# Relative-position bias of a two-layer encoder: stored backward, loaded once, read backward

## Chip, cores and metric

One core of a Trainium2 chip runs the whole kernel as one program. The metric is the device time of one execution in microseconds; the figure compared is the median of several executions.

## What is computed

The reference is two layers of a streaming encoder on 512 tokens of width 1024. Each layer has a feed-forward block, a token mixer with three branches (gated DeltaNet, RG-LRU, chunked band attention), a cross-attention and a second feed-forward block, with a layer norm behind each. The change touches band attention:

```
rel = kj - LA_PAST * CHUNK - qi
bias = rel_table[:, clip(rel, -REL_CLIP, REL_CLIP) + REL_CLIP]     # rel_table (8 heads, 257)
valid = (arange(n)[:, None] - LA_PAST + kj // CHUNK) >= 0
s = where(valid, q @ k.T * 64 ** -0.5 + bias, NEG_INF)
p = softmax(s, axis=-1)
o = p @ v
```

A query adds to each score one entry of its head's table, chosen by the distance from query to key. For a tile of 128 queries (on the partitions) and the 256 keys that end with the tile's own, the bias is a Toeplitz matrix: row q is the table, shifted by q. For keys farther back it is one constant per head.

## The kernel before

Weights come as a stream of units of 128x1024 fp32, four slots deep. SyncE issues the loads. GpSimd splits each unit into a high part (L592) and a low part (L589), and every large product is three matmuls (high by high, low by high, high by low). GpSimd splits the unit for a slot only when `unit_begun` says that the unit behind the slot's former one has begun; the first matmul of each unit on TensorE raises it.

All waits are semaphores written out by hand, and each engine runs its list in order.

In the mixer TensorE computes the projections of queries, keys and values (`att_qk`, `att_v`), turns a few gate rows into columns (L850), and then runs band attention: 8 heads by 4 tiles of queries, n = 0 to 31. It keeps two scores ahead: in turn it issues score n + 2, a quarter of an LRU projection (`lru_part(n + 1)`), and the transposes of the probabilities of n (`turn(n)`, L879). Before the loop stand score 0, score 1 and `lru_part(0)`. Score n reuses the bank of score n - 2 and waits until VectorE has added the bias to that one (`biased`, L1886 and L1884).

VectorE runs, in this order: the memset and the softplus of the gate rows (`delta_rows`, 4x512), two copies of the turned columns (L1996, L1997), the softplus of the LRU rates (`lru_rates_out`, L1924 to L1926, on 128x4 tiles `lam`, the helper at L1837 to L1849), and then its part of attention. `link` puts a wait of the engine for its own last instruction behind an instruction.

The bias tile is made on the device. In layer norm 0 ScalarE's queue loads the gate weights (512 KB), `ba_w` (256 KB) and the table into `ext` (8 KB). VectorE pads `ext` on the left with its first entry (L1853). ScalarE's queue stores `ext` to DRAM (L1705), waits, and loads it back with overlapping rows: partition p of `bias` begins p entries further on, 1 MB in all (L1707). That puts the rows in reversed order, so TensorE multiplies by a flipped identity (L859), into four banks of `aux`, and the banks are copied back over `bias`, two by VectorE (L1859) and two by ScalarE (L1405). VectorE then writes the mask into a corner of the tile (L1863).

Of the kernel before, what the change touches and what calls it, by code (L numbers as in the profile page):

```python
# [41 lines left out]
CH = SEQ // P  # L42
REL = 128
ALPHA = (2 * DEPTH) ** 0.25
LN_EPS = 1e-5
# [131 lines left out]

C_ID, C_CAUSAL, C_FLIP, C_LEVEL = 0, P, 2 * P, 3 * P
CONST = (3 + LEVELS) * P

# [178 lines left out]

def trunk(nc, xT, memT, stream, par_d, ba_w_d, gate_w_d, table_d, const_d, ext_d, outT):  # L360
    with ExitStack() as ctx:
        def sem(name):
            return ctx.enter_context(nc.semaphore(name))

        def sb(name, shape, dt=F32, scope=ctx):
            return scope.enter_context(nc.sbuf_tensor(name, shape, dt))
# [27 lines left out]
        with ExitStack() as mix:  # L394
# [11 lines left out]
            with ExitStack() as att:  # L406
                aq = sb("aq", [P, KB, SEQ], F32, att)
                ak = sb("ak", [P, KB, SEQ], F32, att)
                av = sb("av", [P, CH, BRW], F32, att)
                bias = sb("bias", [P, HA, 2 * P], F32, att)  # L410
                ext = sb("ext", [HA, 3 * P - 1], F32, att)
                sc = sb("sc", [P, CH, SEQ], F32, att)
                pt = sb("pt", [P, CH, SEQ], F32, att)
                neg_max = sb("neg_max", [P, HA * CH], F32, att)
                row_sum = sb("row_sum", [P, HA * CH], F32, att)
                inv_sum = sb("inv_sum", [P, HA * CH], F32, att)
                lc = sb("lc", [P, KB, SEQ], F32, att)
# [39 lines left out]

        ba_w = sc[:, 0, :].rearrange("p (k m) -> p k m", k=KD)
        row_f = pt[0:HN, 0, :]
        tt = tmp[3].rearrange("p (c m) -> p c m", c=CH)  # L460

        ident = const[:, C_ID:C_ID + P]
        flip = const[:, C_FLIP:C_FLIP + P]
        causal = const[:, C_CAUSAL:C_CAUSAL + P]

        def level_mask(s):
# [5 lines left out]
        const_loaded, par_loaded = sem("const_loaded"), sem("par_loaded")  # L472
        mix_par_loaded = [sem(f"mix_par_loaded{n}") for n in range(3)]
        ext_stored, bias_loaded, mem_loaded, out_stored = sem("ext_stored"), sem("bias_loaded"), sem("mem_loaded"), sem("out_stored")
        unit_loaded = [sem(f"unit_loaded{s}") for s in range(SLOTS)]
# [21 lines left out]

        ext_padded = Signal(sem("ext_padded"), 1)
        bias_flipped, bias_copied, bias_copied_late = (
            Signal(sem(n), c) for n, c in (("bias_flipped", 4), ("bias_copied", 2), ("bias_copied_late", 2)))  # L500
        bias_masked = Signal(sem("bias_masked"), 1)
# [114 lines left out]
        def _(pe):  # L616
            def mm(out, w, x, start=True, stop=True):
                return pe.matmul(out, w, x, start=start, stop=stop, skip_group_check=True)  # L618
# [205 lines left out]
            def attention(l):  # L824
# [31 lines left out]

                pe.wait_ge(bias_loaded, l * 16 + 16)
                for m in range(4):
                    mm(aux[:, m, :], flip, bias[:, 2 * m:2 * m + 2, :]).then_inc(bias_flipped.sem, 1)  # L859
                pe.wait_ge(bias_copied.sem, bias_copied.at(l, 2))  # L860

                def score(n):
# [7 lines left out]
                def turn(n):  # L870

                    h, i = divmod(n, CH)
                    pe.wait_ge(probs.sem, probs.at(l, n + 1))
                    if n < 2:
                        pe.wait_ge(bias_copied_late.sem, bias_copied_late.at(l, n + 1))
                    if n >= 2:
                        pe.wait_ge(turned_out.sem, turned_out.at(l, n - 1))
                    for j in range(i + 1):
                        last = pe.transpose(aux[:, 2 + n % 2, j * P:(j + 1) * P], sc[:, i, j * P:(j + 1) * P], ident)  # L879
                    last.then_inc(turned.sem, 1)  # L880
# [436 lines left out]
        def _(act):  # L1317
# [71 lines left out]
            def attention(l):  # L1389
# [13 lines left out]

                for m in range(2):
                    act.wait_ge(bias_flipped.sem, bias_flipped.at(l, m + 3))  # L1405
                    fn(bias[:, 2 * m + 4:2 * m + 6, :], aux[:, m + 2, :].rearrange("p (h k) -> p h k", h=2),
                       ACT.Copy).then_inc(bias_copied_late.sem, 1)

                def turned_copy(n):
# [275 lines left out]
            def mixer_loads(l):  # L1685
                act.dma_start(gate_w[:, :, :, :], gate_w_d[l]).then_inc(mix_par_loaded[0], 16)
                act.dma_start(ba_w, ba_w_d[l]).then_inc(mix_par_loaded[1], 16)
                act.dma_start(ext[:, P - 1:3 * P - 1], table_d[l][:, 0:2 * P]).then_inc(mix_par_loaded[2], 16)

# [5 lines left out]
            for l in range(DEPTH):  # L1695
# [7 lines left out]

                act.wait_ge(ext_padded.sem, ext_padded.at(l, 1))
                act.dma_start(ext_d, ext[:, :]).then_inc(ext_stored, 16)  # L1705
                act.wait_ge(ext_stored, l * 16 + 16)
                act.dma_start(bias[:, :, :], bass.AP(tensor=ext_d.tensor, offset=0,  # L1707
                                                     ap=[[1, P], [3 * P - 1, HA], [1, 2 * P]])).then_inc(bias_loaded, 16)
                attention(l)
# [15 lines left out]
        def _(dve):  # L1725
# [125 lines left out]
            def attention(l):  # L1851
                dve.wait_ge(mix_par_loaded[2], l * 16 + 16)
                dve.tensor_copy(ext[:, 0:P - 1], ext[:, P - 1:P].broadcast_to([HA, P - 1])).then_inc(ext_padded.sem, 1)  # L1853
                lru_rates(l)
                delta_rows(l)
                lru_rates_out(l)
                for m in range(2):
                    dve.wait_ge(bias_flipped.sem, bias_flipped.at(l, m + 1))
                    dve.tensor_copy(bias[:, 2 * m:2 * m + 2, :], aux[:, m, :].rearrange("p (h k) -> p h k", h=2)).then_inc(bias_copied.sem, 1)  # L1859
                dve.wait_ge(bias_copied.sem, bias_copied.at(l, 2))  # L1860
                dve.wait_ge(bias_copied_late.sem, bias_copied_late.at(l, 2))

                dve.memset(bias[0:P // 2, :, 3 * P // 2:2 * P], NEG).then_inc(bias_masked.sem, 1)  # L1863
                dve.wait_ge(bias_masked.sem, bias_masked.at(l, 1))
# [376 lines left out]
def pack(x, mem, ln_g, ln_b, ffn_w12, ffn_w3, mix_w_in, dn_conv_w, dn_a_log, dn_dt_bias, dn_norm_w, lru_conv_w,  # L2241
# [77 lines left out]
    i = np.arange(P)  # L2319
    const = [np.eye(P), i[:, None] <= i[None, :], np.eye(P)[::-1]]  # L2320
    for s in range(LEVELS):
        b = 1 << s
        const.append((i[:, None] // b % 2 == 0) & (i[None, :] // b == i[:, None] // b + 1))
    return {"in_xT": np.ascontiguousarray(A(x)[0].T), "in_memT": np.ascontiguousarray(A(mem)[0].T),
            "in_stream": np.concatenate(stream, 0), "in_par": np.stack(par), "in_ba_w": np.stack(ba),
            "in_gate_w": np.stack(gw), "in_table": A(la_rel_bias), "in_const": np.concatenate(const, 1).astype(np.float32)}

# [14 lines left out]
```

## Time and profile before

| | |
|---|---|
| median of 3 executions | 3166.64 us (3164.72 to 3166.77) |
| profiled execution, first to last instruction | 3165.2 us |
| what lies between that span and the median | 1.4 us |
| TensorE busy | 3110.6 us (98%) |
| VectorE busy | 1471.4 us (46%) |
| ScalarE busy | 720.8 us (23%) |
| GpSimd busy | 1736.3 us (55%) |
| mean granted TensorE clock | 0.992 |

One execution was recorded. Times are microseconds from the span's start, unless marked ns. In a profile PE is the matmul side of TensorE and PEld its weight load, DVE is VectorE, ACT is ScalarE, POOL is GpSimd, SP is SyncE; a name such as ACTq is the engine's DMA queue. The two layers repeat each other some 1571 us apart. L618, L1321 and L1735 are lines of helpers, which stand for all matmuls, all activations and all low parts; there the names of the tiles tell the operations apart.

### The profile page before, as it was taken

The page shows a single profiled execution, that of the slowest core. Times are in us where ns is not written, and L with a number is a line of the kernel's source. Part 1 is how long each engine was busy: PE and PEld are TensorE (multiplying, and loading weights), DVE is VectorE, ACT ScalarE, POOL GpSimd, SP SyncE. Part 2 cuts the span into 40 slices and gives each one's busy share as a digit, 9 for nine tenths or more (in the row PEclk, how much of TensorE's full clock was granted, in tenths as well). Part 3 has the DMA queues.
Part 4 walks back from the last instruction along what each step waited for, and adds up shares of the span by engine and source line. Part 5 has one row for each costly group of instructions (what it writes and reads, how often), then busy time and mean ns, then how long its engine had stood idle before and what let it go on. Part 6 is the DMA issues. An engine that isn't in the chain of part 4 may idle for free.

```text
span 3165.2 us, 42772 instructions
## 1 busy us (share of the span) xinstructions
PE 3110.6 (98%) x15968; PEld 2593.9 (82%) x15968; DVE 1471.4 (46%) x2202; ACT 720.8 (23%) x1433; POOL 1736.3 (55%) x987
## 2 busy tenths in 40 slices
PE   8999999999999999999999999999999999999998
PEld 7888875788888979888888888667888889788887
DVE  3332367755536336332244314677555472353323
ACT  1110224422221423110121103134222224231102
POOL 6666553433346745666656665535333567456664
PEclk9999999999999999999999999999999999999999
DMA  4323221211122322333322332212111224222332
GB/s 155 99 94 106 97 94 40 74 54 54 57 83 87 127 74 87 93 99 100 100 91 96 99 100 92 92 41 74 61 54 51 86 90 130 70 86 94 99 100 67
DMA packets 81173, 272.79 MB, mean 86 GB/s; under 512 B 8433, under 2 KB 16913, under 8 KB 81041
## 3 DMA queue, kind: packets, MB, share of 16 engines
q1 hardware_dynamic: 75808, 264.27, 25.7%
q10 hardware_dynamic: 5088, 5.96, 0.6%
q8 instruction: 100, 1.64, 0.2%
q0 software_dynamic: 144, 0.66, 0.1%
q14 instruction: 33, 0.26, 0.0%
HBM read 268.73 MB, written 2.12 MB: 86 GB/s over the span
## 4 chain that ended last, share of the span: by engine, by line
PE 94%; DVE 3%; ACT 1%; issue 1%; DMA 0%; SPq 0%; ACTq 0%; DVEq 0%
PE acc L618 82%; PE aux L618 12%; PE aux L879 1%; DVE xf L1819 0%; DVE xl L1735 0%; DVE xf L1816 0%; DMA xf<-in_xT 0%; DVE ml L1735 0%; ACT xf L1321 0%; PE aux L1249 0%; DVE xf L1760 0%; DVE y_sum L1774 0%; ACT tmp L1321 0%; ACT xh L1321 0%; DVE lr L2056 0%
## 5 line engine op out<-in xcount | busy, mean ns | idle before, releaser
L589 POOL TENSOR_TENSOR wl<-raw,wh 128x1024 fp32r<-128x1024 f32 x496 | 1213.8, 2449 | 80.1 <-ACT wh L1321 40.1
L592 POOL TENSOR_SCALAR wh<-raw 128x1024 fp32r<-128x1024 f32 x480 | 523.3, 1090 | 1314.2 <-PE acc L618 901.0
L618 PE MATMUL acc<-xh,wh 128*128 128x512 f32 (+1 forms) x2688 | 1016.8, 383 | 17.9 <-ACT xh L1321 15.1
L618 PE MATMUL acc<-xh,wl 128*128 128x512 f32 (+1 forms) x2688 | 987.2, 372 | 0.0
L618 PE MATMUL acc<-xl,wh 128*128 128x512 f32 (+1 forms) x2688 | 948.2, 371 | 0.0
L618 PEld LDWEIGHTS acc<-xh,wh 128*128 128x128 f32 x2688 | 512.9, 191 | 127.0 <-issue 38.7
L618 PEld LDWEIGHTS acc<-xh,wl 128*128 128x128 f32 x2688 | 513.4, 191 | 79.1 <-issue 1.9
L618 PEld LDWEIGHTS acc<-xl,wh 128*128 128x128 f32 x2688 | 488.2, 190 | 87.8
L1735 DVE TENSOR_TENSOR hl<-tmp,hh 128x512 f32 x88 | 238.4, 2709 | 81.8 <-ACT hh L1321 81.8
L618 PE MATMUL acc<-hl,wh 128*128 128x512 f32 (+1 forms) x704 | 264.5, 376 | 0.0
L618 PE MATMUL acc<-hh,wl 128*128 128x512 f32 (+1 forms) x704 | 264.5, 376 | 0.0
L618 PE MATMUL acc<-hh,wh 128*128 128x512 f32 (+1 forms) x704 | 264.5, 376 | 0.0
L1760 DVE SCALAR_TENSOR_TENSOR xf<-acc,xf 128x512 f32<-128x512 f32 (+1 forms) x72 | 43.4, 602 | 399.7 <-PE acc L618 399.4
L1746 DVE TENSOR_TENSOR tmp<-tmp,acc 128x512 f32<-128x512 f32 x88 | 60.5, 688 | 327.5 <-PE acc L618 326.5
L1321 ACT ACTIVATE hh<-tmp 128x512 f32 x88 | 56.0, 637 | 466.3 <-DVE tmp L1746 466.3
L618 PEld LDWEIGHTS acc<-hh,wl 128*128 128x128 f32 x704 | 132.5, 188 | 24.2
L618 PEld LDWEIGHTS acc<-hh,wh 128*128 128x128 f32 x704 | 132.5, 188 | 24.2
L618 PEld LDWEIGHTS acc<-hl,wh 128*128 128x128 f32 x704 | 132.5, 188 | 23.9
L618 PEld LDWEIGHTS aux<-tmp 128*128 128x128 f32 x1088 | 138.8, 195 | 10.5 <-DVE tmp L2151 3.0
L618 PE MATMUL aux<-tmp 128*128 128x128 f32 x1088 | 139.9, 278 | 0.7 <-DVE tmp L2151 0.3
L1321 ACT ACTIVATE tmp<-acc 128x512 f32<-128x512 f32 x96 | 57.4, 598 | 336.0 <-PE acc L618 336.0
L1743 DVE SCALAR_TENSOR_TENSOR tmp<-tmp,acc 128x512 f32<-128x512 f32 x88 | 60.5, 687 | 147.3 <-ACT tmp L1321 147.3
(287 smaller groups left out, 3912.6 us busy)
## 6 DMA issues: line engine op xcount, KB each, us to landing
raw<-in_stream SPq DMA_DIRECT2D x496, 512.0 KB, 3.3
xf<-in_xT SPq DMA_DIRECT2D x2, 1024.0 KB, 10.5
bias<-rel_scratch ACTq DMA_DIRECT2D x2, 1024.0 KB, 6.0
mraw<-in_memT ACTq DMA_DIRECT2D x2, 1024.0 KB, 5.8
out_xT<-xf SPq DMA_DIRECT2D x16, 128.0 KB, 1.7
gate_w<-in_gate_w ACTq DMA_DIRECT2D x2, 512.0 KB, 5.5
const<-in_const POOLq DMA_DIRECT2D x1, 640.0 KB, 6.6
sc<-in_ba_w ACTq DMA_DIRECT2D x2, 256.0 KB, 5.7
```

The costliest lines, as they stand in the source:

```text
L589: pool.tensor_tensor(wl[:, s, :], raw[:, s, :], wh[:, s, :].bitcast(F32), ALU.subtract).then_inc(unit_split, 1)
L592: pool.tensor_scalar(wh[:, s, :], raw[:, s, :], 1.0, 0.0, ALU.mult, ALU.add).then_inc(hi_step, 1)
L618: return pe.matmul(out, w, x, start=start, stop=stop, skip_group_check=True)
L879: last = pe.transpose(aux[:, 2 + n % 2, j * P:(j + 1) * P], sc[:, i, j * P:(j + 1) * P], ident)
L1321: return act.activation(out, in_, func, **kw)
L1735: return tt_(dst, whole, high.bitcast(F32), ALU.subtract)
L1743: stt_(tmp[1][:, :], tmp[0][:, :], 1.0, acc[:, 2 * m, :], ALU.add, ALU.mult).then_inc(freed_d.sem, 1)
L1746: tt_(tmp[2][:, :], tmp[1][:, :], acc[:, 2 * m + 1, :], ALU.mult).then_inc(freed_d.sem, 1)
L1760: evicted = stt_(xf[:, d, t], half_bank(norm, d, half)[:, t], factor, xf[:, d, t], ALU.mult, ALU.add)
```

## The change

The host lays the table out already padded on the left and back to front: `TABLE` = 383 entries per head. One load with overlapping rows, issued in layer norm 0 in the place of the table's load, puts partition p at entry p onward into `bias_back`. `bias` becomes a view of that tile with a negative step on the last axis, so it reads like the old tile. The left padding, the store to DRAM and the load back, the four flipping matmul calls of a layer (which the trace shows as eight matmuls) and the four copies are gone, with their semaphores. The flipped identity leaves the constants (640 to 576 KB). The mask's memset is at the mirrored corner. A filler tile takes the place of `ext`.

```diff
-C_ID, C_CAUSAL, C_FLIP, C_LEVEL = 0, P, 2 * P, 3 * P
-CONST = (3 + LEVELS) * P
+C_ID, C_CAUSAL, C_LEVEL = 0, P, 2 * P
+CONST = (2 + LEVELS) * P
...
-                bias = sb("bias", [P, HA, 2 * P], F32, att)
-                ext = sb("ext", [HA, 3 * P - 1], F32, att)
+                bias_back = sb("bias_back", [P, HA, 2 * P], F32, att)
+                sb("att_fill", [P, 384], F32, att)
...
+        bias = bias_back[:, :, ::-1]
...
-                pe.wait_ge(bias_loaded, l * 16 + 16)
-                for m in range(4):
-                    mm(aux[:, m, :], flip, bias[:, 2 * m:2 * m + 2, :]).then_inc(bias_flipped.sem, 1)
-                pe.wait_ge(bias_copied.sem, bias_copied.at(l, 2))
-
...
-                    if n < 2:
-                        pe.wait_ge(bias_copied_late.sem, bias_copied_late.at(l, n + 1))
...
-                for m in range(2):
-                    act.wait_ge(bias_flipped.sem, bias_flipped.at(l, m + 3))
-                    fn(bias[:, 2 * m + 4:2 * m + 6, :], aux[:, m + 2, :].rearrange("p (h k) -> p h k", h=2),
-                       ACT.Copy).then_inc(bias_copied_late.sem, 1)
...
-                act.dma_start(ext[:, P - 1:3 * P - 1], table_d[l][:, 0:2 * P]).then_inc(mix_par_loaded[2], 16)
+                act.dma_start(bias_back[:, :, :], bass.AP(tensor=table_d.tensor, offset=l * HA * TABLE,
+                                                          ap=[[1, P], [TABLE, HA], [1, 2 * P]])).then_inc(bias_loaded, 16)
...
-                act.wait_ge(ext_padded.sem, ext_padded.at(l, 1))
-                act.dma_start(ext_d, ext[:, :]).then_inc(ext_stored, 16)
-                act.wait_ge(ext_stored, l * 16 + 16)
-                act.dma_start(bias[:, :, :], bass.AP(tensor=ext_d.tensor, offset=0,
-                                                     ap=[[1, P], [3 * P - 1, HA], [1, 2 * P]])).then_inc(bias_loaded, 16)
...
-                dve.wait_ge(mix_par_loaded[2], l * 16 + 16)
-                dve.tensor_copy(ext[:, 0:P - 1], ext[:, P - 1:P].broadcast_to([HA, P - 1])).then_inc(ext_padded.sem, 1)
                 lru_rates(l)
                 delta_rows(l)
                 lru_rates_out(l)
-                for m in range(2):
-                    dve.wait_ge(bias_flipped.sem, bias_flipped.at(l, m + 1))
-                    dve.tensor_copy(bias[:, 2 * m:2 * m + 2, :], aux[:, m, :].rearrange("p (h k) -> p h k", h=2)).then_inc(bias_copied.sem, 1)
-                dve.wait_ge(bias_copied.sem, bias_copied.at(l, 2))
-                dve.wait_ge(bias_copied_late.sem, bias_copied_late.at(l, 2))
-
-                dve.memset(bias[0:P // 2, :, 3 * P // 2:2 * P], NEG).then_inc(bias_masked.sem, 1)
+                dve.wait_ge(bias_loaded, l * 16 + 16)
+
+                dve.memset(bias_back[0:P // 2, :, 0:P // 2], NEG).then_inc(bias_masked.sem, 1)
                 dve.wait_ge(bias_masked.sem, bias_masked.at(l, 1))
...
+    table = A(la_rel_bias)[:, :, np.clip(np.arange(TABLE) - (P - 1), 0, 2 * P - 1)[::-1]]
```

## Rows read from the trace of the kernel before

**Rows 1.** The page's chain of work that ended last: share of the span by engine.
```profile
PE 94%; DVE 3%; ACT 1%; issue 1%; DMA 0%; SPq 0%; ACTq 0%; DVEq 0%
```

**Rows 2.** Timeline, layer 0: start us, us, engine line operation out<-in xcount [idle before <-releaser].
```profile
458.26 3.70 PE L618 MATMUL aux<-bias,const 128*128 128x512 f32 x8 [0.47 <-DVE cols L1997]
...
459.26 1.15 DVE L1846 SCALAR_TENSOR_TENSOR lam<-lam 128x4 f32<-128x4 f32 x6
...
461.24 0.17 DVE L1926 TENSOR_SCALAR lam<-lam 128x4 f32<-128x4 f32 x1
461.32 1.28 DVE L1859 COPY bias<-aux 128x512 f32<-128x512 f32 x2
...
462.65 0.92 PE L618 MATMUL aux<-ak,aq 64*128 64x128 f32 x4 [0.69 <-DVE bias L1859]
...
463.50 0.50 PE L618 MATMUL acc<-xh,wh 128*128 128x512 f32 x1
...
464.18 1.05 POOL L592 TENSOR_SCALAR wh<-raw 128x1024 fp32r<-128x1024 f32 x1 [8.32 <-issue]
...
465.08 0.91 PE L618 MATMUL aux<-ak,aq 64*128 64x384 f32 x2
...
465.31 2.38 POOL L589 TENSOR_TENSOR wl<-raw,wh 128x1024 fp32r<-128x1024 f32 x1
```

**Rows 3.** One stretch of attention: us, busy (count) of PE, PEld, DVE, ACT, POOL; clock, DMA.
```profile
489.00:502.00 13.00, 13.00 (x52) 7.84 (x52) 9.70 (x23) 5.20 (x16) 3.73 (x3) 1.00 0.12 42
```

**Rows 4.** Timeline, the same place in layer 1.
```profile
2032.55 0.17 DVE L1926 TENSOR_SCALAR lam<-lam 128x4 f32<-128x4 f32 x1
...
2034.14 0.48 DVE L1863 MEMSET bias<- 64x512 f32 x1 [0.24 <-ACT bias L1321]
2034.66 0.29 DVE L1886 TENSOR_TENSOR sc<-aux,bias 128x128 f32<-128x128 f32 x1
...
2036.39 0.91 PE L618 MATMUL aux<-ak,aq 64*128 64x384 f32 x2
```

**Rows 5.** Timeline by engine: the softplus of the gate rows, GpSimd's first pair beside it.
```profile
424.97 9.98 DVE L1846 SCALAR_TENSOR_TENSOR tmp<-tmp 4x512 f32<-4x512 f32 x6
434.99 0.68 DVE L1847 SCALAR_TENSOR_TENSOR tmp<-tmp 4x512 f32<-4x512 f32 x1
...
425.14 1.43 POOL L592 TENSOR_SCALAR wh<-raw 128x1024 fp32r<-128x1024 f32 x1 [1.91 <-PE acc L618]
426.65 2.70 POOL L589 TENSOR_TENSOR wl<-raw,wh 128x1024 fp32r<-128x1024 f32 x1
```

**Rows 6.** L1803 by line: duration ns least/median/most, first and last start, form.
```profile
L1803 DVE TENSOR_TENSOR stat<-stat x16: 160/160/771, 371.1 to 3153.6; 128x2 f32<-128x2 f32 x16
```

**Rows 7.** Timeline at two waits of TensorE, and the stretch behind each.
```profile
379.62 0.58 PE L618 MATMUL aux<-mean_w,y_sum 128*128 128x1 f32 x2 [1.70 <-DVE y_sum L1774]
...
1211.22 0.61 PE L618 MATMUL aux<-mean_w,y_sum 128*128 128x1 f32 x4 [1.08 <-DVE y_sum L1774]
...
1212.00:1217.00 5.00, 5.00 (x31) 5.00 (x31) 4.79 (x14) 3.46 (x6) 1.39 (x1) 0.66 0.43 156
381.00:388.00 7.00, 7.00 (x40) 7.00 (x40) 6.07 (x19) 5.11 (x11) 0.80 (x1) 0.62 0.58 189
```

**Rows 8.** Behind norm 0: timeline, a stretch, and DMA issues (KB each, us to landing).
```profile
402.57 1.05 POOL L592 TENSOR_SCALAR wh<-raw 128x1024 fp32r<-128x1024 f32 x1 [20.77 <-PE acc L618]
...
403.82 1.09 ACT L1321 ACTIVATE aq<-acc 128x512 f32<-128x512 f32 x2 [2.47 <-PE acc L618]
...
388.00:412.00 24.00, 24.00 (x168) 20.16 (x168) 10.90 (x31) 11.27 (x22) 9.18 (x6) 1.00 0.27 84
...
bias<-rel_scratch ACTq DMA_DIRECT2D x2, 1024.0 KB, 6.0
...
const<-in_const POOLq DMA_DIRECT2D x1, 640.0 KB, 6.6
```

**Rows 9.** Instructions on the bias tile: duration ns least/median/most.
```profile
L1886 DVE TENSOR_TENSOR sc<-aux,bias x64: 291/414/426, 463.6 to 2129.4; 128x256 f32<-128x256 f32 x48, 128x128 f32<-128x128 f32 x16
...
L1707 ACTq DMA_DIRECT2D bias<-rel_scratch x2: 400/402/403, 403.4 to 1974.7; - x2
```

More of the change, by code:

```diff
@@ L43 @@
 REL = 128
+TABLE = 3 * P - 1
 ALPHA = (2 * DEPTH) ** 0.25
@@ L356, with trunk @@
 LRU_DVE += [(x,) for p in range(KB) for x in ([f"h{p}", f"y{p}"] + ([f"y_lo{p - 1}"] if p else []))] + [(f"y_lo{KB - 1}",)]
-def trunk(nc, xT, memT, stream, par_d, ba_w_d, gate_w_d, table_d, const_d, ext_d, outT):
+def trunk(nc, xT, memT, stream, par_d, ba_w_d, gate_w_d, table_d, const_d, outT):
     with ExitStack() as ctx:
@@ L462, in trunk @@
         ident = const[:, C_ID:C_ID + P]
-        flip = const[:, C_FLIP:C_FLIP + P]
         causal = const[:, C_CAUSAL:C_CAUSAL + P]
@@ L472, in trunk @@
         const_loaded, par_loaded = sem("const_loaded"), sem("par_loaded")
-        mix_par_loaded = [sem(f"mix_par_loaded{n}") for n in range(3)]
-        ext_stored, bias_loaded, mem_loaded, out_stored = sem("ext_stored"), sem("bias_loaded"), sem("mem_loaded"), sem("out_stored")
+        mix_par_loaded = [sem(f"mix_par_loaded{n}") for n in range(2)]
+        bias_loaded, mem_loaded, out_stored = sem("bias_loaded"), sem("mem_loaded"), sem("out_stored")
         unit_loaded = [sem(f"unit_loaded{s}") for s in range(SLOTS)]
@@ L496, in trunk @@
         x_hi, x_lo = (StepSignal(sem(n), LN_ROWS, start=2 * KD) for n in ("x_hi", "x_lo"))
-        ext_padded = Signal(sem("ext_padded"), 1)
-        bias_flipped, bias_copied, bias_copied_late = (
-            Signal(sem(n), c) for n, c in (("bias_flipped", 4), ("bias_copied", 2), ("bias_copied_late", 2)))
         bias_masked = Signal(sem("bias_masked"), 1)
@@ L2319, in pack @@
     i = np.arange(P)
-    const = [np.eye(P), i[:, None] <= i[None, :], np.eye(P)[::-1]]
+    const = [np.eye(P), i[:, None] <= i[None, :]]
     for s in range(LEVELS):
@@ L2323, in pack @@
         const.append((i[:, None] // b % 2 == 0) & (i[None, :] // b == i[:, None] // b + 1))
+    table = A(la_rel_bias)[:, :, np.clip(np.arange(TABLE) - (P - 1), 0, 2 * P - 1)[::-1]]
     return {"in_xT": np.ascontiguousarray(A(x)[0].T), "in_memT": np.ascontiguousarray(A(mem)[0].T),
             "in_stream": np.concatenate(stream, 0), "in_par": np.stack(par), "in_ba_w": np.stack(ba),
-            "in_gate_w": np.stack(gw), "in_table": A(la_rel_bias), "in_const": np.concatenate(const, 1).astype(np.float32)}
+            "in_gate_w": np.stack(gw), "in_table": np.ascontiguousarray(table), "in_const": np.concatenate(const, 1).astype(np.float32)}
 def kernel(**inputs):
@@ L2335 @@
     ins = {n: nc.dram_tensor(n, a.shape, mybir.dt.from_np(a.dtype), kind="ExternalInput").ap() for n, a in arrays.items()}
-    ext_d = nc.dram_tensor("rel_scratch", (HA, 3 * P - 1), F32).ap()
     out = nc.dram_tensor("out_xT", (DM, SEQ), F32, kind="ExternalOutput").ap()
     trunk(nc, ins["in_xT"], ins["in_memT"], ins["in_stream"], ins["in_par"], ins["in_ba_w"], ins["in_gate_w"],
-          ins["in_table"], ins["in_const"], ext_d, out)
+          ins["in_table"], ins["in_const"], out)
     got = run_bass_kernel_spmd(nc, [arrays], core_ids=[0]).results[0]["out_xT"]
```

## The prediction

> **What bounds the kernel now.** I read the page first. Its chain of work that ended last is TensorE for 94% of the span [rows 1], so an edit counts only by what it does to the time at which TensorE starts its next work. The change has two places, one in each layer: the end of the projections, just before the first scores of band attention. There I read the timeline, all engines together, and the reader should follow three of them.
>
> TensorE [rows 2]: the four matmul calls that reverse the bias (eight in the trace) from 458.26, 3.70 us, a wait for the copies, the first two scores at 462.65, the first quarter of the LRU projection (`lru_part(0)`) at 463.50, score 2 at 465.08. VectorE: a chain of small operations on `lam` (`lru_rates_out`, each waits for the one before), of which six equal steps start at 459.26 and the last instruction at 461.24; then copies, the mask's memset and the first biased score. GpSimd: idle, and only at 464.18, 0.68 us after `lru_part(0)` begins, does it split the next weight unit, since it waits for `unit_begun`, which the first matmul of `lru_part(0)` raises. Inside attention TensorE is busy 13.00 of 13.00 us and VectorE 9.70 [rows 3]: VectorE follows, so time that TensorE gains or loses at the start of the stage stays gained or lost.
>
> **Taken away on TensorE.** The scores need the columns that also released the reversal, so they can start at 458.26 instead of 462.65: 4.39 us a layer. After them `lru_part(0)`, which stands 0.85 us behind score 0 [rows 2], starts at 458.26 + 0.85 = 459.11. It and what follows up to score 2 take 465.08 - 463.50 = 1.58 us, so TensorE reaches score 2 at 460.69. Score 2 waits for the first biased score, as it reuses its bank. This is what is late next, and VectorE decides it.
>
> **VectorE, first without GpSimd.** The chain's last instruction stays at 461.24, as the chain starts on the transposed rows. The copy behind it started 0.08 later [rows 2]; now the memset does, at 461.32. Layer 1 shows memset to first biased score as 2034.66 - 2034.14 = 0.52, and 0.29 for the score [rows 4], so that starts at 461.84 and ends at 462.13; score 2 follows at some 462.18 (0.05 for the signal, as between the end of the copies, 461.32 + 1.28, and the scores at 462.65). That would be 2.90 us sooner than 465.08, not 4.39.
>
> **VectorE with GpSimd.** But the reordering wakes GpSimd sooner: 459.11 + 0.68 = 459.79, in the middle of the `lam` chain. What follows has a precedent in this trace, the same softplus over 4x512 rows [rows 5]. Six `scalar_tensor_tensor` there take 9.98 us where one alone takes 0.68, so 0.03 apart they should take 6 x 0.68 + 5 x 0.03 = 4.23. They lose 5.75 us to two pairs of GpSimd operations (the pair shown and one like it 5.4 us later): 2.87 us a pair. Size does not protect: a 128x2 `tensor_tensor` takes 160 ns as a rule and 771 in three places [rows 6]. At 459.79 four of the six steps have begun (459.26 + 0.19 each); two or so slip through between GpSimd's two operations, the remaining five stand until the second lets go. All before the memset shifts by 2.87: first biased score at 464.71, its end 465.00, score 2 at 465.05. In layer 1 the last `lam` step starts at 2032.55, so score 2 comes at 2032.55 + 0.08 + 2.87 + 0.52 + 0.29 + 0.05 = 2036.36, against 2036.39 [rows 4]. So the two places give back 0.03 us each: **0.1 us together**. TensorE has exchanged 3.70 us of matmuls for an idle stretch from 460.69 to 465.05, 4.36 us.
>
> The row says that VectorE gets the path back 2.87 us after a pair. The Trainium skill (SBUF — State Buffer, Who interferes with whom) goes further: a VectorE instruction with two SBUF inputs contends with a GpSimd instruction that reads SBUF, and the first to issue has the shared pair for the whole instruction. Taken with the full length of GpSimd's rows, 1.05 + 2.38 = 3.43 us [rows 2], it would put score 2 another 0.6 us back in each layer, and the sum 1.2 us higher. The trace agrees with the block itself; for its length I stay with the row.
>
> **The clock.** The trace does not show an idle stretch of 4.36 us on TensorE in mid-kernel, so I bound its price by shorter ones [rows 7]. After a wait of 1.08 us that ends at 1211.2 the granted clock is 0.66 over the next stretch of 5 us: the lower level, 1.2 GHz, for 0.34 x 5 x 2 = 3.4 us. After a wait of 1.70 us that ends at 379.6 it is 0.62 over the 7 us from 381, low for 5.3 us. Dense matmuls at half the clock lose half their time: 1.7 us and 2.7 us. Below, nothing, if the clock holds; and a stretch some three times as long as these is nearer to them than to none, so I take 1.9 us a layer, toward the shorter. **Plus 3.8 us**, ends 0 and 5.4.
>
> **The moved load.** ACT issues three loads in the norm as before, the 1 MB bias in place of the 8 KB table, so nothing is added to its queue there (the bias's issue takes 0.4 us [rows 9]). Two issues and the round trip behind the norm go. They held the first `aq` copy, which begins at 403.82 [rows 8] with the queue's last issue just over, but TensorE does not wait for it: it is busy for 24.00 of the 24 us around it, so 0. Landing took 6.0 us for the bias; begun near 384 it has some 75 us until it is used, and GpSimd, idle for 20.77 us up to 402.57, needs no new weights then. Ahead of it in ACT's queue stand the two loads that were ahead before. Cost 0 if hidden; without that cover, 6 us once. The constants shrink by a tenth, a tenth of 6.6 us at most at the start [rows 8]; TensorE waits there for x, not for them, so 0.1 of gain, from 0 to 0.7.
>
> **The backward reads.** 64 `tensor_tensor` on a bank and the bias take 291 to 426 ns [rows 9], about one element a cycle. No row reads backward. Below, no change. Above, at half rate, 0.27 us for 256 columns and 0.13 for 128: 3 x 0.27 + 0.13 = 0.94 us in some 12.7 us of one head, against 13.00 - 9.70 = 3.3 us idle on VectorE. Hidden up to four times the rate. I take 0, except 0.1 a layer for the first one at worst.
>
> **Sum.** The profiled execution spans 3165.2 us, 1.4 below the 3166.64 median; the terms are differences and carry over. 3165.2 - 0.1 + 3.8 - 0.1 = 3168.8 of span, **3170.2 us** of median.
>
> **The rivals.**
> - *VectorE is through in time* (GpSimd's start slips behind the `lam` chain, or the small steps pass). Score 2 comes 2.90 us sooner in both layers: 3166.64 - 5.8 - 0.1 = 3160.7. TensorE still idles 1.5 us, near the 1.08 that cost 1.7, so 3164.1 with the clock. For it: the chain needs only 1.5 us more when GpSimd wakes. Against: the precedent, twice.
> - *The path is blocked but the clock holds*: 3166.5. The change does nothing to the time though it removes 7.4 us of matmuls.
> - *The full gain*, 2 x 4.39 = 8.8 us: 3157.9. It wants VectorE ahead of TensorE, against 461.84 for its first biased score.
> - *Backward reads are slow* (the other side). Past four times the present rate VectorE becomes the bound of attention. At eight times it needs 7 x 0.94 = 6.6 us more per head, 3.3 over the idle, for 16 heads 53 us: 3220. Nothing in the trace speaks for it but that no such read is there.
> - *A low clock of the long kind in both layers, with the longer block*: 5.4 + 1.2 - 0.2 = 6.4, 3173.0, at the edge of slower.
>
> **How the numbers follow.** Forecast (block and low clock) 0.58; block with clock held 0.12; VectorE in time 0.17, half of it with a low clock; full gain 0.03; slow reads 0.03; long low clock 0.07. A difference under 0.2%, 6.3 us, cannot be told from none: 3160.3 to 3173.0. Forecast, held clock and most of the third are inside. Faster takes the full gain and a tenth more of the third, 0.06; slower the last two, 0.1; the same, 0.84. The range 3162.5 to 3173.0 leaves out the third without a low clock (0.08), the full gain, slow reads and the long kind, together under 0.2.
>
> **What the profile after would show.** TensorE: scores at 458.3, `lru_part(0)` at 459.1, then a wait of 4.4 us for a `tensor_tensor` on `sc`. GpSimd: a split starting at 459.8, not 464.2. VectorE: the `lam` steps no longer 0.2 apart but with two stops, 0.8 and 2.1 us. The clock: near 0.5 in the 3.4 us behind the wait. ACT: first `aq` copy earlier with no effect. VectorE's reads of the bias: still 291 and 414 ns. The prediction is wrong if the `lam` steps run undisturbed, if TensorE's wait is under 2 us, or if the clock stays at 1.00.

## The result, and the profile after

The changed kernel takes 3175.4 us in the median of 7 executions (3174.35 to 3177.44), the kernel before 3166.77 (7 executions): 1.003, with a 95% interval of 1.002 to 1.0041. A second comparison gave 3178.53 against 3164.74, 1.0041 (1.0027 to 1.0054). So the change loses 0.3 to 0.4%. The forecast of 3170.2 had the direction right and the size too small, and its range ended at 3173.0.

The profiled execution of 3174.35 us spans 3171.3, 6.1 more than before. Its timeline at the changed place of layer 0 answers to [rows 2]:

```profile
458.89 0.92 PE L616 MATMUL aux<-ak,aq 64*128 64x128 f32 x4 [0.47 <-DVE cols L1973]
...
459.74 0.50 PE L616 MATMUL acc<-xh,wh 128*128 128x512 f32 x1
...
459.89 4.03 DVE L1828 SCALAR_TENSOR_TENSOR lam<-lam 128x4 f32<-128x4 f32 x6
...
460.43 1.05 POOL L590 TENSOR_SCALAR wh<-raw 128x1024 fp32r<-128x1024 f32 x1 [3.94 <-issue]
...
461.56 2.34 POOL L587 TENSOR_TENSOR wl<-raw,wh 128x1024 fp32r<-128x1024 f32 x1
463.95 0.16 DVE L1829 SCALAR_TENSOR_TENSOR lam<-lam 128x4 f32<-128x4 f32 x1
...
464.96 0.48 DVE L1839 MEMSET bias_back<- 64x512 f32 x1
465.48 0.29 DVE L1862 TENSOR_TENSOR sc<-aux,bias_back 128x128 f32<-128x128 f32 x1
...
465.83 1.64 PE L616 MATMUL aux<-ak,aq 64*128 64x384 f32 x2 [4.43 <-DVE sc L1862]
```

The scores and `lru_part(0)` come right behind the turned columns. GpSimd starts 0.69 us behind `lru_part(0)`, in the middle of the six steps. They take 4.03 us for 1.15: 2.88 us lost, where the forecast said 2.87. The steps one by one (duration ns least/median/most, start):

```profile
L1828 DVE SCALAR_TENSOR_TENSOR lam<-lam x6: 161/162/2203, 459.9 to 461.7; 128x4 f32<-128x4 f32 x6
...
L1828 DVE SCALAR_TENSOR_TENSOR lam<-lam x1: 1009/1009/1009, 460.5 to 460.5; 128x4 f32<-128x4 f32 x1
```

The fourth step, from 460.5, takes 1.01 us and ends with GpSimd's first operation; the fifth passes between the two in 0.16; the sixth, from 461.7, takes 2.20 us and ends with the second. So what is lost is the rest of each GpSimd operation from the moment at which VectorE's step began, less the 0.16 us that the step takes anyway; that is why it comes to 2.88 and not to the pair's 3.39 us. TensorE waits 4.43 us, where it said 4.36. Score 2 takes 1.64 us for two matmuls where it took 0.91, at a lower granted clock.

The stretch of 5.2 us behind the wait, and the same in layer 1 (columns as [rows 3]):

```profile
465.80:471.00 5.20, 5.17 (x10) 3.04 (x11) 3.05 (x10) 1.52 (x6) 0.00 (x0) 0.50 0.18 69
...
2041.00:2047.00 6.00, 6.00 (x15) 3.26 (x16) 3.74 (x12) 1.97 (x7) 0.00 (x0) 0.72 0.11 44
```

A granted clock of 0.50 is the lower level, 1.2 GHz. In layer 0 it holds for all the 5.2 us of work; in layer 1 0.72 over 6 us is 0.28 x 6 x 2 = 3.4 us. The kernel before has a granted clock of 1.00 through the whole of attention, in both layers.

TensorE's waits, whole execution (us in total, times, longest), and the instructions on the bias tile, which answer to [rows 9]:

```profile
PE aux L616 <- DVE sc L1862: 8.9, 2, 4.4
...
PE aux L616 <- DVE cols L1973: 1.0, 2, 0.5
```

```profile
L1862 DVE TENSOR_TENSOR sc<-aux,bias_back x64: 292/415/425, 465.5 to 2135.5; 128x256 f32<-128x256 f32 x48, 128x128 f32<-128x128 f32 x16
...
L1674 ACTq DMA_DIRECT2D bias_back<-in_table x2: 456/456/457, 385.0 to 1959.3; - x2
```

Backward reads cost nothing: 292 and 415 ns against 291 and 414. The load with overlapping rows takes 8.5 us to land for 6.0 [rows 8], 70 us ahead of its use. ScalarE's first `aq` copy is no longer held up, and nothing comes of it (timeline):

```profile
402.92 0.60 ACT L1312 ACTIVATE aq<-acc 128x512 f32<-128x512 f32 x1 [0.94 <-PE acc L616]
```

To see where the 6.1 us sit, read the chain of work that ended last, in order of time, at three groups that both kernels have: 192 matmuls of `att_v` and its neighbours ahead of attention, 120 behind it, 240 at the merge behind the delta rule. Before, then after (start us, us, what):

```profile
413.56 43.79 PE acc L618 x192
...
582.59 27.21 PE acc L618 x120
...
925.52 54.48 PE acc L618 x240
...
1984.88 43.79 PE acc L618 x192
...
2153.92 27.21 PE acc L618 x120
...
2498.38 54.45 PE acc L618 x240
```

```profile
414.19 43.79 PE acc L616 x192
...
585.71 27.21 PE acc L616 x120
...
930.29 54.48 PE acc L616 x240
...
1989.24 43.80 PE acc L616 x192
...
2159.99 27.21 PE acc L616 x120
...
2504.51 54.48 PE acc L616 x240
```

I call the distance from the first group of a layer to its second attention, and that from its second to its third the delta stage. Attention grew from 169.03 to 171.52 in layer 0 and from 169.04 to 170.75 in layer 1, 4.2 us. The delta stage grew in layer 0 alone, from 342.93 to 344.58; in layer 1 it was 344.46 before already. The 6.1 us are then 0.63 ahead of layer 0's attention, 2.49 in it, 1.65 in its delta stage, -0.41 from there to layer 1's attention, 1.71 in that, 0.06 in its delta stage, and nothing behind. Attention is what the change explains at once; the delta stage is a question.

### The profile page after: what moved, and what is told of

Read it like the earlier page. It is cut to its first block, busy times and chain, and to the rows that moved or that the text cites. A ratio compares the mean times of both kernels' runs of the same rounds, so it can differ in the third digit from the quotient of the medians.

```text
span 3171.3 us, 42718 instructions
## 1 busy us (share of the span) xinstructions
PE 3111.4 (98%) x15952; PEld 2597.0 (82%) x15952; DVE 1474.2 (46%) x2196; ACT 718.8 (23%) x1429; POOL 1736.2 (55%) x987
## 4 chain that ended last, share of the span: by engine, by line
PE 94%; DVE 3%; issue 1%; ACT 1%; DMA 0%; SPq 0%; ACTq 0%; DVEq 0%
PE acc L616 81%; PE aux L616 12%; PE aux L870 1%; DVE xl L1717 0%; DVE xf L1801 0%; DVE xf L1798 0%; DVE ml L1717 0%; DMA xf<-in_xT 0%; PE aux L1240 0%; DVE lam L1828 0%; ACT xf L1312 0%; DVE xf L1742 0%; DVE y_sum L1756 0%; ACT tmp L1312 0%; DVE lr L2032 0%
```

## Experiments

All are built on the changed kernel unless said otherwise. A median stands beside that of the kernel before on the same chip; "attention" and "delta" are the two distances just read, layer 0 and layer 1, each from one profiled execution.

| kernel | median | before | ratio, 95% interval | attention | delta |
|---|---|---|---|---|---|
| changed, again | 3178.53 | 3164.74 | 1.0041 (1.0027 to 1.0054) | 171.64, 171.27 | 344.56, 344.49 |
| rates_early | 3157.26 | 3164.74 | 0.9975 (0.9966 to 0.9984) | 164.52, 164.49 | 343.02, 342.90 |
| hold_split | 3170.70 | 3164.74 | 1.0017 (1.0008 to 1.0026) | 171.34, 170.67 | 344.58, 344.55 |
| fill_idle | 3167.06 | 3164.74 | 1.0007 (0.9998 to 1.0016) | 169.02, 169.18 | 342.94, 342.92 |
| before, again | 3166.20 | 3166.32 | 0.9999 (0.9990 to 1.0008) | 169.04, 169.08 | 344.41, 342.84 |
| forward_full | 3176.84 | 3166.32 | 1.0034 (1.0022 to 1.0046) | 171.42, 173.88 | 344.55, 344.47 |
| load_alone | 3166.28 | 3166.32 | 1.0003 (0.9994 to 1.0012) | 169.04, 169.10 | 344.54, 342.89 |
| flip_rates_early | 3164.45 | 3166.32 | 0.9999 (0.9990 to 1.0008) | 168.80, 168.81 | 342.91, 342.90 |
| early_l0 | 3166.94 | 3166.15 | 1.0003 (0.9994 to 1.0012) | 164.66, 171.44 | 342.92, 344.60 |
| early_l1 | 3166.86 | 3166.15 | 1.0002 (0.9993 to 1.0011) | 171.41, 164.66 | 344.53, 342.96 |
| fill_half | 3176.34 | 3166.15 | 1.0032 (1.0021 to 1.0043) | 172.34, 173.72 | 344.43, 344.46 |
| hold_fill | 3163.74 | 3166.15 | 0.9993 (0.9984 to 1.0002) | 167.52, 167.53 | 343.08, 344.54 |

**The changed kernel again.**

> The changed kernel as it is, for its spread and for the chip that the other kernels of this call run on. Theory A (VectorE's lam chain is stopped by GpSimd's pair, TensorE idles 4.4 us a layer and its clock falls behind it): 8 to 9 us above the kernel before, score 2 about 5 us behind the end of lru_part(0) in both layers, the lower clock behind both waits. Theory B (much of the loss is chance in where the clock falls elsewhere): the difference shrinks to 4 us or less and the profile shows other places of the lower clock than the first one did.

It came out at 3178.53 us, 13.8 above the kernel before and not 8 to 9. Attention lost 2.6 and 2.2 us, both waits were 4.4 us, and theory A stands for these. Something of theory B may remain: 13.8 us of median against 7.2 of profiled span leave something over (the profiled execution was the shortest of its five, 3175.41 us), which the last experiment looks at.

**The lam chain out of the way (rates_early).** It is the cleanest test, and the version that beats both kernels.

```diff
             def attention(l):
+                act.wait_ge(lam_arg.sem, lam_arg.at(l, 1))
+                fn(lam[:, 2, :], lam[:, 1, :], ACT.Exp, scale=-1.0).then_inc(lam_exp.sem, 1)
                 for n in range(2 * KB):
...
-                act.wait_ge(lam_arg.sem, lam_arg.at(l, 1))
-                fn(lam[:, 2, :], lam[:, 1, :], ACT.Exp, scale=-1.0).then_inc(lam_exp.sem, 1)
...
                 lru_rates(l)
-                delta_rows(l)
                 lru_rates_out(l)
                 dve.wait_ge(bias_loaded, l * 16 + 16)
                 dve.memset(bias_back[0:P // 2, :, 0:P // 2], NEG).then_inc(bias_masked.sem, 1)
                 dve.wait_ge(bias_masked.sem, bias_masked.at(l, 1))
+                delta_rows(l)
```

> The changed kernel with lru_rates_out and the mask's memset ahead of the gate rows, in VectorE's idle time behind norm 0, and ScalarE's exponential of lam ahead of its first aq copy. Theory A: score 2 no longer waits for VectorE; both layers give 4.4 us against the kernel before and the lower clock at these places is gone, so 3166.8 - 8.8 = 3158. Theory B (the backward reads, the moved load or the new addresses cost time wherever they are used): the places gain 8.8 us but the total stays 3 to 5 us above that, 3161 to 3163.

The median is 3157.26, 7.5 us under the kernel before. Timeline of layer 0:

```profile
458.21 0.92 PE L616 MATMUL aux<-ak,aq 64*128 64x128 f32 x4 [0.48 <-DVE cols L1973]
458.73 0.29 DVE L1862 TENSOR_TENSOR sc<-aux,bias_back 128x128 f32<-128x128 f32 x1 [0.58 <-PE aux L616]
...
460.64 0.91 PE L616 MATMUL aux<-ak,aq 64*128 64x384 f32 x2
```

VectorE now waits for the scores instead of the other way round, and score 2 follows `lru_part(0)` without a wait. Attention takes 164.5 us, 4.5 less than before, in both layers: the 4.39 us that the removed work was worth. These are 9.0 us; the medians differ by 7.5, and where the other 1.5 us lie no profile shows. The chain itself is no faster at its new place, where it still meets the splits, but nothing waits for it there (the same timeline, further ahead):

```profile
403.80 2.28 DVE L1826 TENSOR_SCALAR lam<-lam 128x4 f32<-128x4 f32 x1
406.11 6.85 DVE L1828 SCALAR_TENSOR_TENSOR lam<-lam 128x4 f32<-128x4 f32 x6
```

The six steps lose 6.85 - 1.15 = 5.70 us there to two pairs, 2.85 a pair.

**GpSimd held back (hold_split).** TensorE waits for the mask ahead of `lru_part(0)`, so the split cannot start inside the chain.

```diff
                 score(0)
                 score(1)
+                pe.wait_ge(bias_masked.sem, bias_masked.at(l, 1))
                 lru_part(0)
```

> The changed kernel, but TensorE waits for the mask's memset before lru_part(0), so that GpSimd's pair starts only when the lam chain is through. Theory A: the six steps take 1.15 us again instead of 4.03, lru_part(0) starts at about 462.5, score 2 at 464.1 without a wait, 1.6 us a layer better than the kernel before; the wait of 2.7 us in front of lru_part(0) may still bring the lower clock once a layer at 1.7 us: 3163.6 to 3167. Rival (the chain is slow for another reason than GpSimd): the chain takes 5.9 us as in the changed kernel, and the time is over 3177, as lru_part(0) now waits for it too.

The timeline of layer 0:

```profile
459.44 1.15 DVE L1829 SCALAR_TENSOR_TENSOR lam<-lam 128x4 f32<-128x4 f32 x6
...
462.14 0.29 DVE L1863 TENSOR_TENSOR sc<-aux,bias_back 128x128 f32<-128x128 f32 x1
462.16 0.79 PE L616 MATMUL acc<-xh,wh 128*128 128x512 f32 x1 [2.79 <-DVE bias_back L1840]
```

The same six steps on the same data take 1.15 us when GpSimd is idle: the pair of splits is what stops them. The Trainium skill (SBUF — State Buffer, Who interferes with whom) has the rule, an exclusive hold by whichever side issued first; by that rule, the trace agrees, with 4.03 us against 1.15. But the time was 3170.7, worse than the 3163.6 to 3167 expected. TensorE's wait fell from 4.4 to 2.8 us, and `lru_part(0)` begins at the lower level at once (0.79 us for its first matmul instead of 0.50). The same 15 us of layer 0 in the changed kernel, in this one, and in hold_fill, which is told of below (columns as [rows 3]):

```profile
457.00:472.00 15.00, 10.10 (x31) 5.82 (x30) 9.84 (x31) 3.13 (x11) 3.39 (x2) 0.77 0.22 72
...
457.00:472.00 15.00, 11.73 (x32) 6.72 (x31) 7.92 (x32) 2.87 (x10) 3.40 (x2) 0.66 0.23 72
...
457.00:472.00 15.00, 13.65 (x53) 8.14 (x51) 10.19 (x39) 4.31 (x14) 3.44 (x2) 1.00 0.22 72
```

The clock is low for 0.23 x 15 x 2 = 6.9 us in the changed kernel and for 0.34 x 15 x 2 = 10.2 us behind the shorter wait. In layer 1 it is 6.8 us for 3.4. So the shorter wait was followed by more low clock, not less. The wait's length is not what is paid.

**The wait filled (fill_idle), half filled (fill_half), and the held version filled (hold_fill).** The extra matmuls write to a bank that nothing reads at the time.

```diff
                 lru_part(0)
+                for m in range(4):      # fill_half: 2; hold_fill: 2, behind score(1)
+                    mm(aux[:, 3, :], ident, const[:, 0:SEQ])
```

> The changed kernel with four extra 128x512 fp32 matmuls, which nothing reads, behind lru_part(0) and ahead of score 2: 3.7 us of work in the 4.4 us wait. Theory A: score 2 starts where it did, the clock stays at 1.00 in this stage, and the kernel is 2.4 us a layer faster than the changed one, about 4.5 us in all: 3171. Rival (the lower clock there costs nothing, as VectorE sets the pace behind it, or it falls anyway): no difference to the changed kernel, 3175.

The timeline of layer 0 in the filled kernel:

```profile
458.83 4.04 DVE L1830 SCALAR_TENSOR_TENSOR lam<-lam 128x4 f32<-128x4 f32 x6
...
460.18 3.59 PE L616 MATMUL aux<-const 128*128 128x512 f32 x8
...
464.78 0.91 PE L616 MATMUL aux<-ak,aq 64*128 64x384 f32 x2 [1.00 <-DVE sc L1864]
```

The stretch of 6 us behind it (columns as [rows 3]):

```profile
465.00:471.00 6.00, 6.00 (x23) 3.55 (x23) 4.94 (x16) 2.69 (x9) 0.00 (x0) 1.00 0.13 49
```

VectorE is stopped as before and score 2 stands where it stood, but the clock stays at 1.00, 23 matmuls fit in 6 us where the changed kernel had 10 in 5.2, and attention takes 169.0. Work that serves nothing makes the kernel 11.5 us faster than the changed one on the same chip (3167.06 against 3178.53), and 8.3 faster than the 3175.4 of the first comparison, more than the 4.5 expected. Against the kernel before it is a tie, 1.0007 (0.9998 to 1.0016).

> The changed kernel with two of the four extra matmul calls (1.85 us) in the 4.4 us wait, so that 2.5 us stay idle. Theory A (the cost is the clock and not the wait): score 2 at the same place; if a wait of 2.5 us still brings the lower clock, attention takes 170.7 us or more and the median is 3170 to 3175; if not, as fill_idle, 3167. Rival (the cost is proportional to the idle time): half of fill_idle's gain, 3171 to 3172.

The timeline with half the filling:

```profile
461.14 1.88 PE L616 MATMUL aux<-const 128*128 128x512 f32 x4
465.73 0.91 PE L616 MATMUL aux<-ak,aq 64*128 64x384 f32 x2 [2.71 <-DVE sc L1864]
```

And the stretch of 9 us behind it:

```profile
466.00:475.00 9.00, 9.00 (x22) 4.97 (x22) 4.81 (x15) 2.59 (x9) 0.00 (x0) 0.62 0.08 30
```

Half the filling gives nothing: 3176.34 us, above the 3170 to 3175 expected, and attention at 172.3 and 173.7. The wait of 2.7 us leaves score 2 at full speed (0.91 us) and the clock falls behind it, for 0.38 x 9 x 2 = 6.8 us. The cost is not proportional to the idle time: against fill_idle's attention of 169.1 these waits of 2.7 us cost 3.9 us a layer, and those of 4.4 us in the changed kernel 2.4.

> hold_split with two extra matmul calls between score 1 and the wait for the mask, so that the wait shrinks from 2.8 to 0.9 us. Theory A: lru_part(0) and score 2 start where they did in hold_split, 1.6 us a layer sooner than in the kernel before, and now without the lower clock: attention 167.4 us a layer against 169.0, median 3166 - 3.2 = 3163. Rival (the split of the weights beside the first scores costs what the chain gained): attention stays at 169 or more, 3166.

With 0.9 us of wait left (0.88 in layer 0), attention takes 167.5 us, and the median is 3163.74; both as forecast. The median alone does not tell it from the kernel before (0.9984 to 1.0002); attention does, 1.5 us shorter in each layer. So the 1.6 us a layer that hold_split should have won were real, and the clock had eaten them: its attention of 171.0 is 3.5 us above hold_fill's.

**Reads and load (forward_full, load_alone).** The first has the host write the bias out in full, and reads forward.

```diff
-        bias = bias_back[:, :, ::-1]
+        bias = bias_back
...
-                act.dma_start(bias_back[:, :, :], bass.AP(tensor=table_d.tensor, offset=l * HA * TABLE,
-                                                          ap=[[1, P], [TABLE, HA], [1, 2 * P]])).then_inc(bias_loaded, 16)
+                act.dma_start(bias_back[:, :, :], table_d[l]).then_inc(bias_loaded, 16)
...
-                dve.memset(bias_back[0:P // 2, :, 0:P // 2], NEG).then_inc(bias_masked.sem, 1)
+                dve.memset(bias_back[0:P // 2, :, 3 * P // 2:2 * P], NEG).then_inc(bias_masked.sem, 1)
...
-    table = A(la_rel_bias)[:, :, np.clip(np.arange(TABLE) - (P - 1), 0, 2 * P - 1)[::-1]]
+    back = A(la_rel_bias)[:, :, np.clip(np.arange(TABLE) - (P - 1), 0, 2 * P - 1)[::-1]]
+    table = np.stack([back[:, :, p:p + 2 * P][:, :, ::-1] for p in range(P)], 1)
```

> The changed kernel with the bias written out in full by the host (1 MB per layer, 8 KB per partition, read forward), so without backward reads and without overlapping rows in the load. Theory A: nothing of it matters, L1862 keeps 415 ns and 292 ns, and the time is that of the changed kernel, 3175 to 3178. Rival (backward reads or the 1 KB pieces of the load cost): 2 us or more below it, with shorter L1862 rows.

3176.84 us, as the changed kernel, and L1861, the same read, at 290 and 414 ns. The second is the kernel before with only the load changed: the host pads the table, and the padding on VectorE, the store to DRAM and the load from there are gone; the flip and the copies stay.

```diff
-                act.dma_start(ext[:, P - 1:3 * P - 1], table_d[l][:, 0:2 * P]).then_inc(mix_par_loaded[2], 16)
+                act.dma_start(bias[:, :, :], bass.AP(tensor=table_d.tensor, offset=l * HA * (3 * P - 1),
+                                                     ap=[[1, P], [3 * P - 1, HA], [1, 2 * P]])).then_inc(bias_loaded, 16)
...
-                act.wait_ge(ext_padded.sem, ext_padded.at(l, 1))
-                act.dma_start(ext_d, ext[:, :]).then_inc(ext_stored, 16)
-                act.wait_ge(ext_stored, l * 16 + 16)
-                act.dma_start(bias[:, :, :], bass.AP(tensor=ext_d.tensor, offset=0,
-                                                     ap=[[1, P], [3 * P - 1, HA], [1, 2 * P]])).then_inc(bias_loaded, 16)
...
-                dve.wait_ge(mix_par_loaded[2], l * 16 + 16)
-                dve.tensor_copy(ext[:, 0:P - 1], ext[:, P - 1:P].broadcast_to([HA, P - 1])).then_inc(ext_padded.sem, 1)
```

> The kernel before with the load part alone: table padded by the host, one overlapping load in norm 0, no padding copy, no DRAM round trip; the flip, the copies and forward reads stay. Theory A: nothing on TensorE's path changes, so 3165 within 1.5 us. Rival (moving the megabyte beside the weight loads or taking ScalarE's stall away moves the time): a difference of more than 2 us either way.

3166.28 against 3166.32: nothing. Neither the backward reads nor the moved load costs time.

**The order alone (flip_rates_early).** The kernel before with the lam chain at its early place. The two lines on ScalarE move to the head of attention, as in rates_early.

```diff
                 lru_rates(l)
-                delta_rows(l)
                 lru_rates_out(l)
+                delta_rows(l)
```

> The kernel before with lru_rates_out ahead of the gate rows and ScalarE's exponential of lam ahead of its first aq copy, the flip and copies kept. Theory A (rates_early gained because it cleared the way that the removal had laid open): here the lam chain hides under the flip, so the bias copies wait for the flip as before, and the time is 3165 within 1.5 us. Rival (moving the lam chain is a gain by itself): 2 us or more faster, up to the 7.5 us of rates_early.

The ratio is 0.9999, attention 0.24 us shorter in each layer. Moving the chain is worth nothing while the flip covers it; removing the flip loses 9 to 14 us while the chain stands behind it. Together they give 7.5 us.

**The clock of the kernel before.**

> The kernel before, run as a candidate so that the span and the mean granted clock of each run are listed. Theory A (all of the loss is the clock): its runs sit at a mean clock near 0.992, 0.003 above the changed kernel's 0.988 to 0.990, and 0.003 x 3170 = 9.5 us of clock explain the whole difference. Rival (a part of the loss of 8 to 14 us is in no clock): the clocks differ by under 0.002, which explains under 6 us.

Its eleven executions show a mean clock of 0.992 each, those of the changed kernel 0.987 to 0.990. The expectation multiplied the difference by the span: 0.002 to 0.005 x 3170 is 6 to 16 us, enough for all that there is to explain, though with three digits it is a coarse measure. The Trainium skill (TensorE: Matmul & The Clock Gate, HAM oscillation — how this bites in real kernels) tells of a kernel in which TensorE's wait for the next load brings the lower clock back again and again. This case agrees for its two waits of 4.4 us: each has the lower clock behind it, in all six profiles of the changed kernel.

**One layer at a time (early_l0, early_l1).** The early order in one layer, the changed kernel's in the other; ScalarE's two lines go with it in the same way.

```diff
                 lru_rates(l)
+                if l == 0:              # early_l1: l == 1
+                    lru_rates_out(l)
+                    mask()
                 delta_rows(l)
-                lru_rates_out(l)
-                dve.wait_ge(bias_loaded, l * 16 + 16)
...
+                if l != 0:              # early_l1: l != 1
+                    lru_rates_out(l)
+                    mask()
```

`mask()` stands for the wait for the load, the memset and the wait for it. The two runs test a thing seen in the table: the delta stage, which the change does not touch, takes either 342.9 or 344.5 us.

> The changed kernel with the lam chain and the mask moved ahead of the gate rows in layer 0 alone. The profiles so far: from the 192 fp32r matmuls of att_v to the 120 behind attention 169.0 us before, 171.5 to 173.9 with the wait, 164.5 without it; from there to the 240 of the merge 344.5 us in all eight passes behind such a wait, 342.9 in seven of ten others. Theory A with a link (a clock fall in attention moves what comes behind it so that three more falls follow instead of two): 164.5 and 342.9 in layer 0, 171.5 to 174 and 344.5 in layer 1; median half way between rates_early and the changed kernel, 3166 to 3168. Rival (the third fall in the delta stage is chance): 344.5 or 342.9 in either layer without regard to the wait.

> The same in layer 1 alone. Theory A with a link: 171.5 to 174 and 344.5 in layer 0, 164.5 and 342.9 in layer 1; median 3166 to 3168. Rival (chance): no such pairing.

Medians of 3166.94 and 3166.86 lie half way, and the pairing holds in both: 344.60 and 344.53 in the layer with the wait, 342.92 and 342.96 in the other. The difference is one more fall of the clock, of which this stage has two or three. Over all of the kernels in the table and the two first profiles, the layers whose attention had the low clock took 344.4 to 344.6 in 12 of 12 cases, the others in 4 of 16. (Before these two runs it was 3 of 12; the expectation's "seven of ten others" at 342.9 should be nine of twelve.)

**Four more executions of the changed kernel.**

> The changed kernel, one more profile. If the rest of the loss is in attention: where the execution is longer than 3175.4, a layer's attention takes 172.5 to 174 us instead of 171.5, and the delta stage stays 344.5. Rival: attention stays at 171.5 and the rest shows in another stage.

> The changed kernel, one more profile. If the rest of the loss is in attention: where the execution is longer than 3175.4, a layer's attention takes 172.5 to 174 us instead of 171.5. Rival: attention stays at 171.5 and the rest shows in another stage.

> The changed kernel, one more profile. If the rest of the loss is in attention: where the execution is longer than 3175.4, a layer's attention takes 172.5 to 174 us instead of 171.5. Rival: attention stays at 171.5 and the rest shows in another stage.

> The changed kernel, one more profile. If the rest of the loss is in attention: where the execution is longer than 3175.4, a layer's attention takes 172.5 to 174 us instead of 171.5. Rival: attention stays at 171.5 and the rest shows in another stage.

| time | span | clock | attention | delta |
|---|---|---|---|---|
| 3174.11 | 3172.3 | 0.990 | 171.53, 170.57 | 344.60, 344.47 |
| 3175.97 | 3174.0 | 0.989 | 171.45, 171.81 | 344.64, 344.60 |
| 3177.15 | 3175.4 | 0.989 | 171.47, 173.86 | 344.62, 344.54 |
| 3179.04 | 3177.2 | 0.987 | 171.42, 171.31 | 344.59, 344.57 |

The third has its surplus in attention, as expected. The second and the fourth, also longer than 3175.4, have not. In the fourth the clock is low for longer at the mix output and the norm behind it, and at the same places of layer 1.

```profile
1040.00:1048.00 8.00, 7.96 (x41) 7.96 (x42) 7.04 (x20) 5.58 (x11) 2.21 (x1) 0.57 0.36 123
1217.00:1226.00 9.00, 8.45 (x45) 8.45 (x46) 8.04 (x22) 5.84 (x13) 2.64 (x2) 0.62 0.37 118
```

0.43 x 8 x 2 = 6.9 and 0.38 x 9 x 2 = 6.8 us of low clock, twice what the first profile had at either. So in this execution the rest is the clock as well, but in stages that the change does not touch.

## Why the prediction was wrong

- **What TensorE gains** (removed products, scores at once): right. rates_early collects it, 4.5 us a layer for 4.39.
- **VectorE decides, and GpSimd stops it**: right to a tenth of a microsecond, 2.88 for 2.87 us, a wait of 4.43 for 4.36. Against the turned columns (458.04 before, 458.67 after) score 2 came 7.16 us later for 7.04, so 0.1 us a layer worse than before instead of 0.03 better. The longer block of a full 3.43 us did not come, since VectorE's steps began within GpSimd's operations and ended with them.
- **The clock** is the step that failed: its price, "I take 1.9 us a layer, toward the shorter", 3.8 in all. Inside attention it was too small. Six profiles of the changed kernel show attention at 171.55 us in the mean of twelve passes, 2.5 above the 169.05 of before, or 2.4 without the 0.1 of the later score: 4.8 us for 3.8, with single passes from 1.5 to 4.8. The mean is still inside the term's ends of 0 and 5.4; a single pass is not held by the 2.7 a layer, which was taken from waits of 1.1 and 1.7 us. Pricing a wait by its length did not hold either: waits of 2.7 and 2.8 us cost 3.9 and 3.5 us a layer, in two passes each.
- **What was left out** is the larger part: the same step put the stages behind at nothing, without a reason. The delta stage takes 344.57 us in the mean of the same twelve passes against 343.68 of six of the flipping kernels (before, before again, load_alone): 1.8 us. The mean span is 3173.8 against 3165.0, 8.8 us: 5.0 from attention, 1.8 from the delta stage, and 2.0 from elsewhere. Of these 2.0, 0.9 lie ahead of layer 0's attention, where the changed kernel with its wait filled, or with the chain moved, starts as early as the kernel before (413.1 and 413.5 us), so this part looks like chance. The other 1.1, at the mix outputs and norms behind, come mostly from the second and fourth of the four extra profiles. The rival "a low clock of the long kind", at 0.07, was nearest in its number, 3173.0, but the longer block that it adds was not there.
- **Moved load, backward reads**: right, at nothing (load_alone, forward_full). The smaller constants, forecast at 0.1, were in no run by themselves; they landed in 6.1 us for 6.6, too little to be told apart.
- The span's distance to the execution's time was 1.8 to 3.2 us in the changed kernel's executions, for 1.4 assumed and 1.8 in the eleven executions of the kernel before; that is up to one or two microseconds that no row explains.
- One sum in the chances is slightly off: what the range leaves out adds up to 0.08 + 0.03 + 0.03 + 0.07 = 0.21, not to under 0.2.

**What stays open.** Why an earlier fall makes the third fall of the delta stage certain, when it comes in 4 of 16 cases without one, and why a low clock at the same place is sometimes twice or three times as long, was not settled. At attention in the changed kernel it lasted 6.8 us in nine of twelve passes, 3.4 in two and 10.2 in one. The early_l0 and early_l1 pair shows the link, not its mechanism; a shift in time of what follows is the obvious candidate and was only argued. Nor does any run show a wait at this place between 1.0 us, which cost nothing in fill_idle, and 2.7 us, which cost no less than 4.4 did.

## What to carry to other kernels

Before taking work off the bounding engine, ask what its instructions were covering: here 3.7 us of matmuls hid a chain of tiny VectorE steps, and without them GpSimd set off sooner and stopped this chain for another 2.9 us. Move the covered chain first, into idle time; only the two edits together gave the 7.5 us. And price a new idle stretch on TensorE by what the clock does behind it and in the stages that follow, not by its own length: filling it with useless matmuls was worth more than shortening it from 4.4 to 2.8 us.

## What the runs showed of the hardware that was not expected

- A wait of 2.7 to 2.8 us among dense matmuls cost no less clock than one of 4.4 us, on the mean even more: 3.5 us a layer in hold_split (171.0 against 167.5 in hold_fill) and 3.9 in fill_half (173.0 against 169.1 in fill_idle), two passes each, for 2.4 in the changed kernel (171.55 against 169.1, twelve passes, single ones up to 4.8).
- Waits of 0.9 and 1.0 us there cost nothing (attention 167.5 and 169.1, granted clock 1.00). At the norms waits of 1.08 and 1.70 us had the lower clock behind them [rows 7], so the length of a wait alone does not decide.
- VectorE reads an fp32 operand in SBUF with step -1 beside one in PSUM at the speed of a forward read: 415 against 414 ns for 128x256 (the median of 64 reads, 48 of them of this form).
- A load of 1 MB with overlapping rows of 1 KB, from a table of 12 KB, took 8.5 us to land, the one before, issued at another time, 6.0. The overlap is not the reason: forward_full's load of 1 MB without it, issued at the same place, took 8.4.
- On the 128x4 tiles of the lam chain, 0.16 us a step, a pair of GpSimd operations of 1.05 and 2.34 us stops VectorE for 2.88 us; on 4x512 tiles, 0.68 us a step, it was 2.87 a pair. Two steps stretched to 1.01 and 2.20 us, each until GpSimd's operation ended.
